# A streaming encoder's FFN loop: weight-block sums moved from GpSimd to Vector, Scalar's order changed, once-a-layer pieces moved to the ends of turns

## Chip, cores and metric

One core of one Trainium2 chip runs the whole program. The metric is the device time of one execution in microseconds (us), lower is better.

## What is computed

One inference step of a 2-layer hybrid encoder over 1088 tokens (1024 of a new stream, 64 of a running one), model width 1024, all in float32. Each layer has three token mixers fed by one input projection, an output projection with a residual, and then the part that this case is about, a SwiGLU FFN of width 2816:

```python
h2 = rmsnorm(x, lp['norm_ffn']) * (1.0 + sc2) + sh2
a, u = jnp.split(h2 @ lp['w_ffn_in'], 2, axis=-1)
x = x + g2 * ((jax.nn.silu(a) * u) @ lp['w_ffn_out'])
```

## The kernel before

**Precision.** TensorE works on float32 data split into two parts: a high part that Scalar makes with a copy, and the rest, a low part that Vector makes by subtracting. Each product then is three passes (`PASSES`: high x high, high x low, low x high). So every weight block costs one Scalar copy (`w_high`, L1706; `out_high`, L1712, for the output weights) and one Vector subtraction (`w_low`, L3198; `out_low`, L3202).

**The FFN in turns.** A layer's FFN is 22 turns: two passes over the tokens (`p` = 0 and 1, 544 tokens each, as two halves of 272) times eleven groups of 256 hidden columns. The document counts the turns 0 to 21 in the first layer and 22 to 43 in the second, from the start of product 1a to the next turn's. In a turn the product of the (1024 x 256) block "a" with the tokens, and the same for block "u", are each done as seven products of half blocks instead of eight (Strassen's scheme in Winograd's form). `PRODUCT` tells for each of the seven its weight set, its set of token sums and its PSUM bank, `PE_ORDER` (L78) the order of the fourteen on TensorE, `BANK_FREE` (L79) what frees each one's bank. A product is 12 matmuls of 272 columns. Then the output part (`part`) adds the (256 x 1024) block of the output weights in 16 pieces x0 to x15 of 6 matmuls; a turn has 264 matmuls in all.

**The seven weight sets.** Sets 0, 3 and 5 are quarters of the raw block in SBUF. Sets 1, 2, 4 and 6 are sums: S1 = q10 + q11, S2 = S1 - q00, S3 = q00 - q10, S4 = q01 - S2. GpSimd makes them (`w_step`, L1039): for u at a turn's begin, for the next turn's a in its middle. Each set's place is shared by a and u (but for set 6) and is free once the product that read it is done (`set_free`). Scalar then copies the high part, Vector subtracts.

**Vector, Scalar and GpSimd in a turn** each run a fixed list, written out in their `group` functions (L1044, L1724, L3277). Besides the weights: Scalar copies product banks to SBUF (`kept`: p1a, u2a, p1u, u3a, u2u, u3u), applies Silu (`gated`, s21a) and copies the hidden activations' high parts (g11 ...). Vector adds two products (`summed`: c11a ...), makes the hidden low parts (h11 ...) and the 16 additions to x (`added`, L3300). GpSimd multiplies Silu(a) by u (`times`, L1050: m11u, m22u, m12u). Every wait is a semaphore; an engine stands at a wait with all that is behind it.

**SyncE** (L699 to L704) loads the raw blocks with one buffer for each of a, output weights and u: block a of the next turn once `l5` of the present one (the low part of set 5, last on Vector's list for that block) is made, then the output block after `f3`, then u.

**Once-a-layer pieces.** They are hooked into single turns by name (`hook`): in turn 0 the rest of the first token sums (T3, T4, B22 and their parts); in turn 1 the squares of the last token chunk with GpSimd's additions; in turn 2 the root; in turns 3 and 4 the normalised second half (`scaled` on Vector, `shifted` on Scalar); in turn 10 the token sums T1, T2, T4 and parts B11, B21 for the second pass; in turn 11 as in turn 0; in turn 12 of the first layer the next layer's squares. `Fori` loops run turns 5 to 9 and 13 to 20. In turn 10 the last sets of block a are left to turn 11.

Of the kernel before, what the change touches and what calls it, by code (L numbers as in the profile page):

```python
# [77 lines left out]
PE_ORDER = ["1a", "5a", "2a", "6a", "1u", "7a", "2u", "5u", "6u", "4a", "7u", "3a", "4u", "3u"]  # L78
BANK_FREE = {"1a": ("ffn_dve", -1, "x12"), "5a": ("ffn_dve", -1, "x14"), "2a": ("ffn_dve", -1, "x13"),  # L79
# [94 lines left out]
def program(nc, io, plan):  # L174
# [340 lines left out]
    with ctx:  # L515
# [211 lines left out]
        def _(pool):  # L727
# [23 lines left out]
            for l in range(DEPTH):  # L751
# [272 lines left out]
                def w_step(b, turn, name, first=False):  # L1024
                    s = st(f"fw{b}_pool")
                    i = int(name[1])
                    to = {1: 1, 2: 2, 3: 4, 4: 6}[i]
                    pool.wait_ge(raw_ld[1 + (b == "u")], w_ready(b, turn))
                    set_free(pool, b, turn, to)
                    if first:  # L1030
                        wait(pool, "wo_pe", l, "o19" if to < 4 else "o21")
                    if i == 2:
                        wait(pool, f"fw{b}_pool", turn, "S1")
                    elif i == 4:
                        wait(pool, f"fw{b}_pool", turn, "S2")
                    x, y, op = {1: (w_quarter(b, 1, 0), w_quarter(b, 1, 1), ALU.add), 2: (w_sum(1, b), w_quarter(b, 0, 0), ALU.subtract),
                                3: (w_quarter(b, 0, 0), w_quarter(b, 1, 0), ALU.subtract),
                                4: (w_quarter(b, 0, 1), w_sum(2, b), ALU.subtract)}[i]
                    s.done(V.tensor_tensor(w_sum(to, b), x, y, op), name)  # L1039

                def w_ready(b, turn):
                    return raw_ready(l, 16 + (b == "u")) + 16 * (turn - 2 * l * NGROUP)

                def group(g, hook=lambda name: None, last=False):  # L1044
# [2410 lines left out]
```

How the kernel before makes its waits and increments, by code:

```python
    def wait(eng, name, turn, step):  # L449
        s = st(name)
        eng.wait_ge(s.sem, s.value(turn, step))
# [73 lines left out]
        @block.sync  # L525
# [7 lines left out]
                    wait(sp, "in_pe", 0, "x0b")  # L533
                sp.dma_start(x_rows(t)[0:TILES[t][1]], rows(xp, xs, t)).then_inc(x_ld[t], 16)
            def load_raw(l, n, src, k):
                r = n % 3
                dst = WR[:, r, 0:k * src.shape[-1]].rearrange("p (k c) -> p k c", k=k)
                sp.dma_start(dst, src).then_inc(raw_ld[r], 16)
            for l in range(DEPTH):
                sp.wait_ge(w_lo, l * SPLIT_N + 1)
                if l:
                    for b in "au":
                        wait(sp, f"fw{b}_dve", last_group(l - 1), "l5")
# [16 lines left out]
                    elif l == 0 and n == 2:  # L563
                        wait(sp, "in_pe", 0, "x5b")
                    load_raw(l, n, wl[:, :, FM_COLS[n]:FM_COLS[n] + 256], 8)
                order = [("t", 0), ("t", 1), ("m", 0), ("t", 2), ("t", 3), ("w", 9), ("w", 10), ("w", 11)]
                for kind, n in order:
                    if kind == "m":
                        wait(sp, "n1_dve", l, "lo27")
                        load_mod(sp, l, n)
                    elif kind == "t":
                        sp.wait_ge(w_lo, lo_val(l, n + 1))
                        at = 0
                        for c, wd in TM_SLOTS[n]:
                            sp.dma_start(WTR[:, n % 2].rearrange("p (k c) -> p k c", k=8)[:, :, at:at + wd],
```

## Time and profile before

| | |
|---|---|
| median of 3 runs | 3280.22 us (3276.21 to 3283.54) |
| the profiled execution's own time | 3277.33 us |
| its span, first to last instruction | 3274.9 us |
| TensorE (PE) busy | 3088.1 us, 94% |
| Vector (DVE) busy | 2203.0 us, 67% |
| Scalar (ACT) busy | 1426.2 us, 44% |
| GpSimd (POOL) busy | 1326.2 us, 40% |
| mean granted TensorE clock | 0.986 |

PE is TensorE's matmul, PEld its weight load, SPq SyncE's queue. Matmuls are pipelined, so PE busy isn't PE at its peak: how long TensorE needs is read from the distance between turns. L1912 is the helper through which all matmuls go. The first layer's FFN begins at 885 us of the span, the second's at 2491 us.

### The profile page before, as it was taken

The numbers are of one execution on the slowest core, as the hardware profiler recorded it, in microseconds if no ns is written. First come the engines' busy times: TensorE is split into PE (matmuls) and PEld (weight loads), VectorE is DVE, ScalarE is ACT, GpSimd is POOL, SyncE is SP. The second block draws the span as 40 slices with busy tenths as digits, with TensorE's granted clock in tenths as the row PEclk, the third lists the DMA queues.
The fourth block names the chain that finished last, engine by engine and source line by source line (L and its number), as shares of the span: only waits on it lengthen the run. The fifth ranks groups of instructions, "written<-read, shape, count | busy, mean of one in ns | idle before, by whom it ended". The sixth has DMA issues, their size and how long they took to land. (4 is left out here: it accounts for less than half of the span.)

```text
span 3274.9 us, 61123 instructions
## 1 busy us (share of the span) xinstructions
PE 3088.1 (94%) x21870; PEld 2768.8 (85%) x21870; DVE 2203.0 (67%) x3741; ACT 1426.2 (44%) x3199; POOL 1326.2 (40%) x1439
## 2 busy tenths in 40 slices
PE   6999998999999998999989999898999999999999
PEld 5997666767999998999989976666699999989999
DVE  5312656656588888888873036665557888888986
ACT  5222345444345444444452234554434544444444
POOL 2213556521354354444421145664213543443442
PEclk8999989999999999999999999999999999999999
DMA  6415811104023222223232263111211232222222
GB/s 220 141 68 178 256 42 56 43 17 133 13 91 104 90 90 87 82 90 102 77 110 99 86 218 101 55 53 29 99 52 52 78 100 93 78 89 96 85 102 93
DMA packets 241018, 307.08 MB, mean 94 GB/s; under 512 B 19705, under 2 KB 206414, under 8 KB 240814
## 3 DMA queue, kind: packets, MB, share of 16 engines
q1 hardware_dynamic: 185900, 227.65, 21.2%
q10 hardware_dynamic: 44354, 45.25, 4.3%
q0 software_dynamic: 10560, 31.44, 2.7%
q8 instruction: 130, 2.13, 0.3%
q14 instruction: 74, 0.61, 0.1%
HBM read 264.74 MB, written 39.56 MB: 93 GB/s over the span
## 5 line engine op out<-in xcount | busy, mean ns | idle before, releaser
L1912 PE MATMUL banks<-act_split,w_sets_first 128*128 128x272 f32 x4224 | 554.8, 290 | 15.3 <-DVE w_sets_first L3198 10.4
L1912 PEld LDWEIGHTS banks<-act_split,w_sets_first 128*128 128x128 f32 x4224 | 542.2, 189 | 19.4 <-DVE w_sets_first L3198 13.7
L1912 PE MATMUL banks<-hidden_split,w_out_split 128*128 128x272 f32 x4224 | 541.5, 288 | 5.0 <-DVE x L3300 3.6
L1912 PEld LDWEIGHTS banks<-hidden_split,w_out_split 128*128 128x128 f32 x4224 | 533.5, 188 | 7.3 <-DVE x L3300 6.0
L1912 PE MATMUL banks<-act_split,w_sets_last 128*128 128x272 f32 x3168 | 429.6, 292 | 35.1 <-ACT product_sums L1731 26.8
L1912 PEld LDWEIGHTS banks<-act_split,w_sets_last 128*128 128x128 f32 x3168 | 409.7, 190 | 46.8 <-issue 35.8
L3300 DVE SCALAR_TENSOR_TENSOR x<-banks,mod,x 128x272 f32<-128x272 f32 (+1 forms) x880 | 346.4, 435 | 76.1 <-PE banks L1912 75.5
L1039 POOL TENSOR_TENSOR w_sums_first<-w_raw 128x512 f32<-128x512 f32 x88 | 143.8, 1634 | 566.6 <-PE banks L1912 565.7
L1912 PE MATMUL banks<-act_split,w_split 128*128 128x384 f32 (+1 forms) x2016 | 344.9, 331 | 11.0 <-DVE act_split L2708 10.7
L1912 PEld LDWEIGHTS banks<-act_split,w_split 128*128 128x128 f32 x2016 | 337.6, 191 | 15.5 <-issue 10.6
L1912 PE MATMUL banks<-w_split_tm,act_split 128*128 128x396 f32 (+1 forms) x1728 | 317.2, 344 | 0.0
L1912 PEld LDWEIGHTS banks<-w_split_tm,act_split 128*128 128x128 f32 (+1 forms) x1728 | 300.9, 182 | 13.2 <-issue 4.0
L1712 ACT ACTIVATE w_out_split<-w_raw 128x512 fp32r<-128x512 f32 x176 | 105.4, 622 | 325.4 <-PE banks L1912 325.4
L3202 DVE TENSOR_TENSOR w_out_split<-w_raw,w_out_split 128x512 fp32r<-128x512 f32 x176 | 228.1, 1296 | 0.0
L1050 POOL TENSOR_TENSOR silu_a<-silu_a,product_sums 128x272 f32<-128x272 f32 x132 | 129.1, 978 | 177.2 <-DVE product_sums L3284 168.5
L3198 DVE TENSOR_TENSOR w_sets_first<-w_sums_first,w_sets_first 128x512 fp32r<-128x512 f32 x176 | 192.7, 1095 | 12.0 <-POOL w_sums_first L1039 8.7
L1912 PE MATMUL banks<-k_t,q_t 98*128 98x512 f32 (+4 forms) x448 | 167.3, 487 | 14.2 <-ACT probs L1405 6.3
L3198 DVE TENSOR_TENSOR w_sets_first<-w_raw,w_sets_first 128x512 fp32r<-128x512 f32 x176 | 130.8, 744 | 72.1 <-ACT w_sets_first L1706 72.1
L2937 DVE COPY_PREDICATED r_p<-r_cst,banks 128x512 f32<-128x512 int32 x126 | 112.8, 895 | 90.6 <-PE banks L1912 76.1
L1912 PE MATMUL banks<-r_qb,r_kb 128*128 128x128 f32 x756 | 137.8, 319 | 29.6 <-issue 9.8
L811 POOL TENSOR_TENSOR r_kb<-r_qkg,r_e 128x192 f32<-128x192 f32 x126 | 81.6, 648 | 203.1 <-ACT r_e L1278 159.6
L1912 PEld LDWEIGHTS banks<-r_qb,r_kb 128*128 128x128 f32 x756 | 98.7, 192 | 75.0 <-issue 40.0
(286 smaller groups left out, 5250.5 us busy)
## 6 DMA issues: line engine op xcount, KB each, us to landing
w_raw<-in_w_ffn_in SPq DMA_DIRECT2D x88, 1024.0 KB, 5.1
w_raw<-in_w_ffn_out SPq DMA_DIRECT2D x44, 1024.0 KB, 5.0
w_mod_front<-in_w_mod ACTq DMA_DIRECT2D x50, 512.0 KB, 6.2
w_mod_third<-in_w_mod ACTq DMA_DIRECT2D x26, 512.0 KB, 5.7
z_token_major<-z_stage POOLq DMA_DIRECT2D x64, 198.0 KB, 2.2
r_qkg<-z_feature_major SPq DMA_DIRECT2D x16, 576.0 KB, 4.2
r_v<-z_token_major SPq DMA_DIRECT2D x16, 512.0 KB, 3.7
w_raw<-in_w_o SPq DMA_DIRECT2D x8, 1024.0 KB, 6.3
```

The costliest lines, as they stand in the source:

```text
L811: rstep(V.tensor_tensor(blk(rKB[:, r])[:, :, :, 0:b], blk(rZ[:, g % 2, 3:6])[:, :, :, 0:b], blk(ee)[:, :, :, 0:b], ALU.mult), f"k{g}_{lv}")
L1039: s.done(V.tensor_tensor(w_sum(to, b), x, y, op), name)
L1050: s.done(V.tensor_tensor(SIL[:, i], SIL[:, i], PU[:, j], ALU.mult), f"m{name}u")
L1712: st("fwo_act").done(S.activation(WO2[:, 0, 512 * j:512 * j + 512], WR[:, 0, 512 * j:512 * j + 512], ACT.Copy), f"f{j}")
L1912: return T.matmul(out, lhsT, rhs, start=start, stop=stop, skip_group_check=True)
L2937: rstep(V.copy_predicated(out, mask.unsqueeze(1).broadcast_to([P, 8, 64 // b, b]), src), f"m{g}_{lv}")
L3198: st(f"fw{b}_dve").done(V.tensor_tensor(lo, src, hi.bitcast(F32), ALU.subtract), f"l{i}")
L3202: st("fwo_dve").done(V.tensor_tensor(WO2[:, 1, 512 * j:512 * j + 512], WR[:, 0, 512 * j:512 * j + 512], WO2[:, 0, 512 * j:512 * j + 512].b ...
L3300: ins = V.scalar_tensor_tensor(out=x, in0=ps[OUT_ROT[q % 6]][:, a0:a1], scalar=MOD[:, 40 + d, m:m + 1], in1=x, op0=ALU.mult, op1=ALU.add)
```

## The change

- GpSimd's `group` keeps only the three `times`; the eight sums a turn go to Vector as `w_add`, with the same waits.
- Scalar: `w_high` u1 and u3 and the bank copy u2a stand ahead of s11a, u2 and u6 ahead of p1u, and the next turn's a0 right behind p1u, ahead of out_high 3 and u3a (before: after g11). The other a copies move forward too; s22a goes behind u2u.
- Vector: a new order, with the a sums and most a splits ahead of the output part.
- On TensorE product 2u goes ahead of 7a.
- Once-a-layer pieces: squares, GpSimd's adds and Scalar's `shifted` at the end of their turn, Vector's `scaled` after x3, x6, x9, x12; in turns 0 and 11 the splits a6 and a5 after c11u (before: after u3), T4's low part after c22a, B22's after a1; in turn 10 the passes spread over the turn.

The diff, cut to what matters:

```diff
-PE_ORDER = ["1a", "5a", "2a", "6a", "1u", "7a", "2u", "5u", "6u", "4a", "7u", "3a", "4u", "3u"]
+PE_ORDER = ["1a", "5a", "2a", "6a", "1u", "2u", "7a", "5u", "6u", "4a", "7u", "3a", "4u", "3u"]
...
-                    for name in ("S1", "S2"):
-                        w_step("u", g, name)
-                    hook("S2")
-                    for name in ("S4", "S3"):
-                        w_step("u", g, name)
                     times("11", 0, 0)
...
                     times("22", 3, 2)
...
                     times("12", 1, 0)
...
+                for i in range(2):
+                    group(g0 + i)
+                last_adds()
...
+                for i in range(NGROUP - 1, NGROUP + 2):
                     group(g0 + i)
-                group(g0 + NGROUP + 1, next_adds)
+                if l + 1 < DEPTH:
+                    norm_adds(l + 1, 0)
...
                     w_high("u", g, 0)
                     hook("u0")
                     out_high(g, 2)
+                    w_high("u", g, 1)
                     w_high("u", g, 3)
+                    kept("u2a", "6a", 1, ("ffn_dve", g - 1, "c12a"))
                     gated("11", 0)
-                    w_high("u", g, 1)
-                    kept("u2a", "6a", 1, ("ffn_dve", g - 1, "c12a"))
+                    w_high("u", g, 2)
+                    w_high("u", g, 6)
+                    kept("p1u", "1u", 0, ("ffn_dve", g, "c11a"))
+                    if not last:
+                        w_high("a", g + 1, 0)
                     out_high(g, 3)
-                    kept("p1u", "1u", 0, ("ffn_dve", g, "c11a"))
-                    w_high("u", g, 2)
                     kept("u3a", "7a", 2, ("ffn_pool", g - 1, "m22u"))
-                    w_high("u", g, 6)
-                    gated("22", 3)
                     w_high("u", g, 4)
                     hidden("11", 0, ("ffn_pool", g, "m11u"))
                     if not last:
-                        w_high("a", g + 1, 0)
+                        w_high("a", g + 1, 3)
+                        w_high("a", g + 1, 1)
                     kept("u2u", "6u", 0, ("ffn_pool", g, "m11u"))
+                    gated("22", 3)
...
+                def w_add(b, turn, name, first=False):
+                    to = {"S1": 1, "S2": 2, "S3": 4, "S4": 6}[name]
+                    dve.wait_ge(raw_ld[1 + (b == "u")], w_ready(b, turn))
+                    set_free(dve, b, turn, to)
...
+                    if name in ("S2", "S4"):
+                        own(f"fw{b}_dve", turn, "S1" if name == "S2" else "S2")
...
+                    st(f"fw{b}_dve").done(V.tensor_tensor(w_sum(to, b), x, y, op), name)
...
                     hook("start")
+                    out_low(g, 0)
                     w_low("u", g, 0)
-                    hook("u0")
-                    out_low(g, 0)
+                    w_add("u", g, "S1")
+                    out_low(g, 1)
                     summed("c11a", 0, 0, 1, ("ffn_act", g, "p1a"), ("ffn_pe", g, "2a"))
-                    out_low(g, 1)
                     w_low("u", g, 3)
                     hook("u3")
+                    w_add("u", g, "S2")
+                    w_add("u", g, "S4")
+                    w_low("u", g, 1)
+                    w_low("u", g, 2)
+                    w_low("u", g, 6)
+                    summed("c11u", 0, 0, 4, ("ffn_act", g, "p1u"), ("ffn_pe", g, "2u"))
+                    if not last:
+                        w_low("a", g + 1, 0)
                     out_low(g, 2)
-                    w_low("u", g, 1)
+                    w_add("u", g, "S3")
                     summed("c22a", 3, 2, 2, ("ffn_act", g, "u3a"))
...
                     out_low(g, 3)
                     if not last:
-                        w_low("a", g + 1, 0)
-                    hook("a0")
+                        w_add("a", g + 1, "S1")
+                    w_low("u", g, 4)
+                    hidden("11", 0)
+                    if not last:
+                        w_add("a", g + 1, "S2")
+                        w_low("a", g + 1, 3)
+                        w_low("a", g + 1, 1)
+                    hook("a1")
                     w_low("u", g, 5)
+                    if not last:
+                        w_add("a", g + 1, "S3")
                     summed("c22u", 2, 2, 5, ("ffn_act", g, "u3u"))
...
+                    for q in range(1, 16):
                         added(q)
-                        if not last and q in (5, 8) or q in lows:
-                            w_low("a", g + 1, {5: 2, 8: 4, 10: 6, 13: 5}[q])
+                        if q == 5 and late:
+                            w_low("a", g + 1, 5)
...
                 def set_end(p, name):
                     if name == "start":
                         h_add(p, "T3")
-                    elif name == "u0":
+                    elif name == "u3":
                         h_low(p, "T3")
-                    elif name == "u3":
-                        h_low(p, "T4")
+                    elif name == "c11u":
                         for i in (6, 5):
                             w_low("a", (2 * l + p) * NGROUP, i)
                     elif name == "c22a":
+                        h_low(p, "T4")
+                    elif name == "a1":
                         h_low(p, "B22")
...
                 def pieces_of(k0):
                     def at(name):
-                        if name in ("u0", "u3", "c22a", "c11u"):
+                        if name in ("x3", "x6", "x9", "x12"):
...
                 def turn_over(name):
                     if name == "h11":
                         h_add(1, "T1")
-                    elif name == "a0":
+                    elif name == "a1":
                         h_add(1, "T2")
-                    elif name == "c12a":
+                    elif name == "h22":
                         h_low(1, "B11")
-                    elif name == "h12":
+                    elif name == "x3":
                         h_low(1, "T1")
-                    elif name == "x4":
+                    elif name == "x6":
                         h_add(1, "T4")
-                    elif name == "x7":
+                    elif name == "x9":
                         h_low(1, "B21")
-                    elif name == "x11":
+                    elif name == "x12":
                         h_low(1, "T2")
```

## Rows read from the trace of the kernel before

**Rows 1.** The page, part 1: busy time (share of the span) and instructions per engine

```profile
PE 3088.1 (94%) x21870; PEld 2768.8 (85%) x21870; DVE 2203.0 (67%) x3741; ACT 1426.2 (44%) x3199; POOL 1326.2 (40%) x1439
```

**Rows 2.** Windows: stretch, length; busy PE, PEld, DVE, ACT, POOL; granted clock; DMA share, GB/s

```profile
885.31:927.94 42.63, 36.61 (x266) 36.00 (x265) 40.45 (x59) 19.45 (x36) 19.26 (x11) 0.92 0.23 75
927.94:964.44 36.50, 34.23 (x266) 33.41 (x265) 29.65 (x45) 17.83 (x40) 22.54 (x18) 1.00 0.25 87
...
998.15:1035.02 36.87, 34.17 (x266) 33.35 (x265) 32.23 (x58) 20.16 (x45) 15.69 (x11) 1.00 0.26 87
1035.02:1072.31 37.29, 34.44 (x267) 33.40 (x265) 33.03 (x58) 18.85 (x44) 15.55 (x11) 1.00 0.25 86
1206.48:1240.03 33.55, 33.46 (x267) 33.25 (x265) 29.12 (x46) 15.18 (x32) 15.15 (x11) 1.00 0.28 94
1240.03:1281.19 41.16, 34.62 (x267) 33.41 (x265) 34.00 (x50) 20.21 (x38) 16.68 (x11) 1.00 0.23 77
1281.19:1319.67 38.48, 34.28 (x264) 33.43 (x265) 35.67 (x59) 16.70 (x33) 14.65 (x11) 1.00 0.25 83
1319.67:1357.44 37.77, 34.68 (x269) 33.61 (x267) 31.43 (x52) 18.32 (x41) 23.57 (x18) 1.00 0.25 84
...
899.50:902.40 2.90, 2.86 (x13) 2.89 (x14) 2.90 (x5) 2.22 (x4) 0.00 (x0) 0.50 0.02 6
```

**Rows 3.** Timeline of turn 9: start, length, engine, line, operation, [idle before <-releaser]

```profile
1208.28 0.40 ACT L1731 ACTIVATE product_sums<-banks 128x272 f32<-128x272 f32 x1 [0.44 <-PE banks L1912]
...
1218.54 1.86 DVE L3198 TENSOR_TENSOR w_sets_last<-w_sums_last,w_sets_last 128x512 fp32r<-128x512 f32 x2
1218.79 1.06 POOL L1050 TENSOR_TENSOR silu_a<-silu_a,product_sums 128x272 f32<-128x272 f32 x1 [1.07 <-DVE product_sums L3284]
...
1224.07 0.68 DVE L3198 TENSOR_TENSOR w_sets_last<-w_raw,w_sets_last 128x512 fp32r<-128x512 f32 x1
...
1224.87 3.06 PEld L1912 LDWEIGHTS banks<-act_split,w_sets_last 128*128 128x128 f32 x24 [0.30 <-issue]
...
1231.60 1.72 DVE L3300 SCALAR_TENSOR_TENSOR x<-banks,mod,x 128x272 f32<-128x272 f32 x4
```

**Rows 4.** Groups by line over the whole span: count | busy, mean ns | idle before

```profile
L3202 DVE TENSOR_TENSOR w_out_split<-w_raw,w_out_split 128x512 fp32r<-128x512 f32 x176 | 228.1, 1296 | 0.0
L3198 DVE TENSOR_TENSOR w_sets_first<-w_sums_first,w_sets_first 128x512 fp32r<-128x512 f32 x176 | 192.7, 1095 | 12.0 <-POOL w_sums_first L1039 8.7 <-POOL w_sums_last L1039 2.7
...
L1039 POOL TENSOR_TENSOR w_sums_first<-w_raw 128x512 f32<-128x512 f32 x88 | 143.8, 1634 | 566.6 <-PE banks L1912 565.7 <-DMA w_raw<-in_w_ffn_in 0.9
...
L1712 ACT ACTIVATE w_out_split<-w_raw 128x512 fp32r<-128x512 f32 x176 | 105.4, 622 | 325.4 <-PE banks L1912 325.4
```

**Rows 5.** Timeline before and in turn 0

```profile
877.95 1.28 DVE L3198 TENSOR_TENSOR w_sets_first<-w_raw,w_sets_first 128x512 fp32r<-128x512 f32 x2
...
899.54 3.06 PE L1912 MATMUL banks<-act_split,w_sets_last 128*128 128x272 f32 x12 [4.90 <-ACT product_sums L1731]
...
901.64 0.39 SPq L539 DMA_DIRECT2D w_raw<-in_w_ffn_in  x1
```

**Rows 6.** Timeline: turn 1, then turn 3, then turn 4

```profile
956.63 1.91 POOL L1086 TENSOR_TENSOR norm_sum_n<-norm_sum_n,norm_sq 128x320 f32<-128x320 f32 x2
...
1003.60 1.28 ACT L1736 ACT_TABLE_LOAD   x1
...
1048.56 0.62 DVE L3188 SCALAR_TENSOR_TENSOR h_second<-x,gain_scale,norm_rs_last 128x208 f32<-128x208 f32 x2
```

**Rows 7.** Timeline of turns 10 and 11

```profile
1258.97 1.28 DVE L3222 TENSOR_TENSOR act_f<-h_second,act_f 128x1088 f32<-128x1088 f32 x1
...
1261.03 34.16 SPq L539 DMA_DIRECT2D w_raw<-in_w_ffn_in  x2
...
1262.34 3.24 PE L1912 MATMUL banks<-act_split,w_sets_last 128*128 128x272 f32 x24 [3.13 <-ACT product_sums L1731]
...
1299.97 1.29 POOL L1039 TENSOR_TENSOR w_sums_first<-w_raw 128x512 f32<-128x512 f32 x1 [0.41 <-DMA w_raw<-in_w_ffn_in]
```

More of the change, by code:

```diff
@@ L1022, in add, with group @@
                                f"ad{c}_{d}")
[L1024 to L1044, printed above, removed]
+                def group(g):
                     s = st("ffn_pool")
@@ L1703, in w_high @@
                     else:
[L1704 removed]
+                        wait(act, f"fw{b}_dve", turn, {1: "S1", 2: "S2", 4: "S3", 6: "S4"}[i])
                         src = w_sum(i, b)
@@ L1779, in group @@
                     if not last:
-                        w_high("a", g + 1, 2)
+                        w_high("a", g + 1, 5)
                     hidden("12", 1, ("ffn_pool", g, "m12u"))
-                    if not last:
-                        for i in (6, 4, 5):
-                            w_high("a", g + 1, i)
                     hook("end")
@@ L1836, in squares @@
                 def squares(name):
-                    at = ("p1a", "s11a", "s22a", "g11", "u2u", "g21", "g22", "g12")
-                    if name in at:
-                        last_square(at.index(name))
+                    if name == "end":
+                        for d in range(KT8):
+                            last_square(d)
                 def rooted(name):
@@ L1846, in at @@
                     def at(name):
-                        if name in ("s11a", "p1u", "g11", "u2u"):
-                            k = k0 + ("s11a", "p1u", "g11", "u2u").index(name)
-                            for u in range(2):
-                                shifted(k, 1, u)
+                        if name == "end":
+                            for k in range(k0, k0 + 4):
+                                for u in range(2):
+                                    shifted(k, 1, u)
                     return at
                 def turn_over(name):
-                    if name in ("u3a", "g11", "u2u", "s21a"):
-                        h_high(1, {"u3a": "B11", "g11": "B21", "u2u": "T1", "s21a": "T2"}[name])
+                    if name in ("p1u", "u3a", "u3u", "end"):
+                        h_high(1, {"p1u": "B11", "u3a": "B21", "u3u": "T1", "end": "T2"}[name])
                 def again(name):
@@ L1860, in next_squares @@
                 def next_squares(name):
-                    at = ("p1a", "s11a", "s22a", "g11", "u2u", "g21", "g22", "g12")
-                    if l + 1 < DEPTH and name in at:
-                        normed_square(l + 1, 0, at.index(name))
+                    if l + 1 < DEPTH and name == "end":
+                        for d in range(KT8):
+                            normed_square(l + 1, 0, d)
                 def ending(name):
@@ L3262, in _ @@
                 project(19)
-                for i in (0, 3):
-                    w_low("a", g0, i)
+                w_low("a", g0, 0)
+                w_add("a", g0, "S1", True)
+                w_add("a", g0, "S2", True)
                 h_low(0, "B11")
@@ L3275, in _, with group @@
                 h_low(0, "T2")
-                def group(g, p, hook=lambda name: None, last=False, lows=(10, 13)):
+                def group(g, p, hook=lambda name: None, last=False, late=True):
                     s = st("ffn_dve")
```

97 lines of the change are left out of this document (40 added, 57 removed), and 4 rows, old and new, of the table BANK_FREE.

## Prediction, made before the changed kernel was run

> Times inside a turn count from its first product's start. Products are named as in `PE_ORDER`, sets as in `w_set`.
>
> **What bounds the kernel now.** First the page: TensorE is busy 94% of the span [rows 1], so Vector or Scalar work that is removed only counts where TensorE waits. So I cut the FFN into its 44 turns and read the length of each [rows 2]. Every turn has 264 matmuls of the same size. A turn of the loops (turn 9) takes 33.55 us. Its only wait is the 0.30 us before 4u [rows 3]; of that about 0.25 is excess in the pace of the matmuls, so a turn without waits would take 33.3. The other rows show what the once-a-layer work costs: turn 0 is 9.3 longer than that, turn 1 3.2, turn 3 3.6, turn 4 4.0, turn 10 7.9, turn 11 5.2, turn 12 4.5. The second layer has the same pattern within 0.5 us, except that its turn 12 has nothing extra. So about 75 us stand at the edges and 7 us (29 turns of 0.25) in the steady turns. More than these 80 us the change can't give.
>
> **The price of a sum.** A GpSimd sum takes 1634 ns [rows 4], and while it runs a Vector operation with both inputs in SBUF stands still: the split of a sum takes 1095 ns in the mean [rows 4], two take 1.86 us beside a GpSimd operation [rows 3], and 1.28 without one [rows 5]. Alone it is 0.68 [rows 3], and 0.60 from start to start in a row. No row shows a sum on Vector. It has the shape and operands of the split, so I take 0.60; the bounds are 0.60 and the contended 1.095. Eight per turn are 4.8 us, of which the lost contention pays most: (1296-680)x4 for the output weights [rows 4] and (1095-680)x4 for the split of sums are 4.1 us. Vector is busy 29.1 of 33.55 us in turn 9 [rows 2], so it ends about where it was. The Trainium skill, page VectorE: DVE Perf Modes, section "The DRAIN you can't avoid", says that the next operation doesn't start until the pipe is empty. By it a sum costs 0.68; six operations stand between product 2u and the last sum that matters, and 7u would come some 0.15 us late. The 1.28 us for two [rows 5] speak against it.
>
> **A steady turn after the change.** I walk Vector's new order with 0.60 for each 128x512, 0.35 to 0.4 for the 272-wide ones, and 0.28 from a product's end to who waits for it (1a ends at 1.52, its copy starts at 1.80 [rows 3]). With one product each 1.52 us: `w_low` u0 ends 3.4, c11a 5.5, u3 6.1 (2u starts at 7.6), S2 and S4 at 7.7, u1 8.3, u2 8.9, u6 9.5, c11u 9.9. GpSimd's product takes 1.06 [rows 3] and holds a0 up to 11.0; then out_low 11.6, S3 12.2, c22a 12.6, out_low 13.2, S1 of the next set 13.8. Scalar's `w_high` a1 waits for that S1: 14.4, then its copy u2u ends at 14.8, and 7u, which needs the bank, starts at 15.2: slack 0.35. Vector goes on: u4 14.4, h11, S2, a3, a1, u5 at 17.2, and 4u starts at 18.3: slack 1.0 where it waits now. h21 is there at 22.1, needed at 22.9. In the output part the 16 additions take 0.41 each (four in 1.72 [rows 3]) against TensorE's 0.76: no wait. So 29 turns give 0.25 each: **7.2 us**. The swap of 7a and 2u gives 7a's copy and sum 1.5 us more and costs nothing here, since u3 is early.
>
> **Scalar's copies ahead of its waits, pieces at the ends.** Scalar stands idle before a turn's first copy for 325.4 us in 44 turns [rows 4], 7.4 us each. Turn 1: squares and GpSimd's adds (two in 1.91 [rows 6]) go there, eight of about 1.1 end before the next turn: 3.2 saved. Turn 3: the table load of 1.28 [rows 6] no longer stands ahead of u2a, which 7a waits for; it makes u2u late by 0.7. The pieces of the norm on Vector (0.41 like the additions of that width, and 0.55 for the second half in two parts, 0.62 to its end [rows 6]) come between additions: four pairs are 3.9 us, so x14 comes 0.4 late for the next turn's 5a. Turn 3 becomes 34.4, 2.5 saved. Turn 4 has the 0.4 alone: 3.6 saved. Turn 10: the 1088-wide passes cost 1.28 alone [rows 7] and, like all others, some 0.08 less in a row, 1.2. Two stand before u5, which ends at 20.0: 4u waits 1.8 instead of 3.13 [rows 7], 7u no more; four among the additions put x12 at 35.7, and turn 11 starts at 35.8 instead of 41.2: 5.4 saved. Turn 12, first layer: the adds end about when the norm's matmul wants them, a wait of 0.5: 3.9 saved. The sum over both layers is 6.4+5.0+7.2+10.8+3.9 = **33.3 us**.
>
> **What the same move costs.** At turn 0 and turn 11, `w_low` of a5 and a6 is late by design, and SyncE loads the next "a" block only after a5's. Now that load is issued 13.6 us into turn 11 (the first of the pair at 1261.03 is the "u" block, the second ends its issue at 1295.19) and lands some 5 us later: GpSimd's sum waits for it until 1299.97 [rows 7]. Nobody on Scalar waits, because `w_high` of the next a0 stands behind u3a and g11. After the change it stands right behind p1u, ahead of out_high 3, u3a and u4. Turn 11: Vector starts at 2.4 (x15), T3, a4, out_low, u0, S1, out_low, c11a, u3, T3's low part 9.2, S2, S4, u1, u2, u6, c11u 12.6, a6 and a5 13.8. The load lands at 19.1; Scalar and Vector both stand until then. a0 20.4, out_low, S3, c22a 22.0, T4's low part 23.2: 4a starts at 23.35 instead of the 14.3 when TensorE is free, **a wait of 9 us**. Behind it B22's low part ends at 28.4, which 3a waits for, and the output part begins at 33.1, 11.8 later than in a clean turn. So 45.1 instead of 38.5: 6.6 lost. Turn 0: the pieces before it no longer run beside GpSimd's sums, which pays for the four sums on Vector; 7a no longer waits 4.90 [rows 5]; l5 comes at 901.1, the load lands at 906.5 (issue now 901.64 [rows 5]), and the same chain begins the output part at 920.5 instead of 915.9: 4.6 lost. Twice both: **22.4 us**. A wait of 9 us will also lower TensorE's clock: after the 4.90 us one the granted clock is 0.50 [rows 2], the 1.2 GHz level. Two slow products of 2.7 instead of 1.5 fit almost into the next wait (for 3a, 1.45 us); 0.25 each, 1 us in all. The Trainium skill, TensorE: Matmul & The Clock Gate, "HAM oscillation", has it that idle gaps bring the clock down each time; by it all four waits do, which is what I count.
>
> **Sum.** 7.2+33.3-22.4-1.0 = 17 us off the profiled execution's 3277.3: 3260. The median of the three runs is 2.9 above that, so 3263.
>
> **The rivals.**
> *The late load isn't in the way* (0.11). If the a block is there when Scalar comes to it, turns 0 and 11 lose their 5.5 us of standing each: 22 off, 3241. Against it: a5's release and the 5 us are in the rows, and nothing shortens them.
> *The edges give nothing* (0.15). In turns 3, 4 and 10 Vector has more work than room, and pieces put among additions make those late, as x already is in turn 10 of before. If half of the 33 us stays away, 3280: within 0.2%, about what a measurement of this kernel can tell from no change.
> *The steady turn gets a new wait* (0.09). Place: 7u, through S1 of the next set, `w_high` a1 and u2u on Scalar. Five sums stand before it, the slack is 0.35. At 0.60 each there is no wait; with d more per sum 7u is 5d-0.35 late, in 29 turns. From d = 0.2 on the gain is gone (19 us); at 0.3, well below the contended price (1.095), it is 33 us: 3296, slower. For it: two-input operations are what GpSimd's remaining products hold up. Against it: with the sums gone GpSimd runs 3 operations of 1 us a turn instead of 11.
> *The clock* alone moves nothing: were the slow products never hidden, four times 2.6 make 10 us, 3273, within my own case.
> That the change doesn't do what it says I give nothing: GpSimd's sums are gone from the code.
>
> **How the numbers follow.** My case has 0.65, its own range 3248 to 3276. It lies on the faster side but for its last edge, 0.03, which goes to "same". Faster by over 0.2% (6.6 us): 0.62+0.11 and a little of the second rival, 0.75; same 0.15; slower 0.10. The range reaches to the first rival and to the half gain: 3240 to 3283.
>
> **What the changed profile would show.** Right: loop turns of 33.3 without a wait before 4u; Vector's sums at 0.68 each, splits of sums and output weights near 0.68; GpSimd down to 3 operations a turn; turn 10 near 36; in turns 0 and 11 a TensorE wait of about 9 us before 4a, with Scalar's a0 copy waiting for the DMA of w_raw, and a low clock after it. Wrong: a wait before 7u in every loop turn, sums of 0.9 or more, turns 3 and 4 not under 36, or turn 11 under 40.

## The result, and the profile after

The changed kernel takes **3255.92 us** (median of 4 runs, 3253.46 to 3256.22), the kernel before 3279.19 us (4 runs, 3276.21 to 3283.54): a ratio of **0.9935**, with a 95% interval of 0.9923 to 0.9947. The forecast was 3263, with a range of 3240 to 3283 and 0.75 for "faster": right in sign, inside its range, and 7 us short of the gain. The profiled execution took 3256.1 us, its span is 3253.6 against 3274.9.

Part 1 of the page of the kernel after, as in [rows 1]:

```profile
PE 3073.5 (94%) x21870; PEld 2768.3 (85%) x21870; DVE 2205.9 (68%) x4093; ACT 1448.5 (45%) x3199; POOL 759.6 (23%) x1087
```

GpSimd lost 352 instructions and 567 us of busy time. Vector took the 352 over, and its busy time rose by 3 us only: the sums cost it 253 us, and what it already did became 250 us shorter. That is the exchange that the prediction worked out. Groups of the kernel after by line (lines have moved: L3172 is the split of a set, before L3198; L3176 that of the output weights, before L3202; L3166 a sum on Vector; L1030 GpSimd's product, L1664 Scalar's `w_high`):

```profile
L3172 DVE TENSOR_TENSOR w_sets_last<-w_sums_last,w_sets_last 128x512 fp32r<-128x512 f32 x176 | 143.3, 814 | 0.0
L3176 DVE TENSOR_TENSOR w_out_split<-w_raw,w_out_split 128x512 fp32r<-128x512 f32 x176 | 141.5, 804 | 4.4 <-ACT w_out_split L1670 3.1
L1030 POOL TENSOR_TENSOR silu_a<-silu_a,product_sums 128x272 f32<-128x272 f32 x132 | 118.9, 900 | 1395.7 <-DVE product_sums L3262 1395.7
L3172 DVE TENSOR_TENSOR w_sets_first<-w_sums_first,w_sets_first 128x512 fp32r<-128x512 f32 x176 | 116.8, 683 | 1.0 <-ACT w_sets_first L1664 1.0
L1664 ACT ACTIVATE w_sets_first<-w_raw 128x512 fp32r<-128x512 f32 x176 | 109.9, 625 | 35.5 <-DMA w_raw<-in_w_ffn_in 32.9 <-PE banks L1871 1.7
L3166 DVE TENSOR_TENSOR w_sums_last<-w_raw,w_sums_first 128x512 f32<-128x512 f32 x88 | 71.4, 812 | 3.3
L3166 DVE TENSOR_TENSOR w_sums_first<-w_raw 128x512 f32<-128x512 f32 x88 | 60.2, 684 | 0.0
```

Three of the four sums cost 684 to 688 ns. S4 (`w_sums_last<-w_raw,w_sums_first`) costs 812 in the mean: 42 of its 88 run beside a GpSimd product, at 942 each, the other 46 take 692. The split of a first-half sum fell from 1095 to 683 ns and that of the output weights from 1296 to 804 [rows 4]; what is above 683 in the first and second row is those groups' share beside GpSimd's remaining products (about 1.21 us for 44 and 1.23 for 38 of the 176; 0.68 to 0.69 for the others). Windows of the kernel after, turns 0, 1, 3, 4, 8, 10, 11 and 12 of the first layer, columns as in [rows 2]:

```profile
881.32:929.30 47.98, 36.53 (x266) 35.35 (x265) 38.99 (x64) 19.60 (x36) 2.82 (x3) 0.89 0.26 88
929.30:962.48 33.18, 33.18 (x266) 33.18 (x265) 29.48 (x53) 19.01 (x40) 9.25 (x10) 1.00 0.29 96
996.20:1029.95 33.75, 33.41 (x266) 33.22 (x265) 30.99 (x62) 20.48 (x43) 2.83 (x3) 1.00 0.28 95
1029.95:1063.13 33.18, 33.18 (x266) 33.18 (x265) 31.88 (x66) 20.22 (x45) 2.83 (x3) 1.00 0.29 97
1162.67:1195.85 33.18, 33.18 (x266) 33.18 (x265) 29.03 (x53) 15.55 (x32) 2.66 (x3) 1.00 0.29 95
1229.03:1265.06 36.03, 33.79 (x266) 33.23 (x265) 32.99 (x55) 20.09 (x38) 2.44 (x3) 1.00 0.18 59
1265.06:1310.78 45.72, 36.09 (x265) 35.70 (x265) 37.88 (x70) 17.77 (x34) 2.83 (x3) 0.89 0.28 93
1310.78:1344.31 33.53, 33.53 (x269) 33.40 (x267) 30.27 (x63) 19.60 (x41) 10.22 (x10) 1.00 0.29 95
```

Timeline of the loop turn 8 (from 1162.67): c11u, S1 of the next set, and Scalar's copy u2u.

```profile
1172.16 0.43 DVE L3262 TENSOR_TENSOR product_sums<-product_sums,banks 128x272 f32<-128x272 f32 x1
...
1175.85 0.68 DVE L3166 TENSOR_TENSOR w_sums_first<-w_raw 128x512 f32<-128x512 f32 x1
...
1177.10 0.38 ACT L1689 ACTIVATE product_sums<-banks 128x272 f32<-128x272 f32 x1
```

In a loop turn TensorE is busy for all of its 33.18 us. Turns 1 and 4 are as short as that, turns 3 and 12 nearly so, and turn 10 became 5.1 us shorter. Turns 0 and 11 alone became longer, by 5.3 and 7.2 us, at a granted clock of 0.89. The two layers together, all 44 turns: 25.4 us lost in turns 0, 11, 22 and 33, 45.6 us won in the others, **20.2 us** net.

The timeline of turn 11 (it starts at 1265.06) shows where its time went:

```profile
1277.22 0.43 DVE L3262 TENSOR_TENSOR product_sums<-product_sums,banks 128x272 f32<-128x272 f32 x1
...
1279.60 0.38 SPq L539 DMA_DIRECT2D w_raw<-in_w_ffn_in  x1
...
1284.59 0.63 ACT L1664 ACTIVATE w_sets_first<-w_raw 128x512 fp32r<-128x512 f32 x1 [8.15 <-DMA w_raw<-in_w_ffn_in]
1285.13 0.61 ACT L1670 ACTIVATE w_out_split<-w_raw 128x512 fp32r<-128x512 f32 x1
1285.26 0.69 DVE L3172 TENSOR_TENSOR w_sets_first<-w_raw,w_sets_first 128x512 fp32r<-128x512 f32 x1 [5.83 <-ACT w_sets_first L1664]
...
1287.41 1.29 DVE L3204 TENSOR_TENSOR act_split<-act_f,act_split 128x1088 fp32r<-128x1088 f32 x1
...
1288.80 10.09 PE L1871 MATMUL banks<-act_split,w_sets_last 128*128 128x272 f32 x60 [9.35 <-DVE act_split L3204]
```

The next "a" block's load is issued 14.5 us into the turn and Scalar's a0 gets it 5.0 us later. Scalar stood 8.15 us for it, then Vector 5.83; the split of T4, which product 4a reads, comes last, and TensorE stands 9.35 us.

### The profile page after: what moved, and what is told of

Its sections match the earlier page's. It is cut to its first block and busy times, and to the rows that moved or that the text cites. A ratio compares the mean times of both kernels' runs of the same rounds, so it can differ in the third digit from the quotient of the medians.

```text
span 3253.6 us, 60947 instructions
## 1 busy us (share of the span) xinstructions
PE 3073.5 (94%) x21870; PEld 2768.3 (85%) x21870; DVE 2205.9 (68%) x4093; ACT 1448.5 (45%) x3199; POOL 759.6 (23%) x1087
## 5 line engine op out<-in xcount | busy, mean ns | idle before, releaser
L1871 PE MATMUL banks<-act_split,w_sets_last 128*128 128x272 f32 x3168 | 422.9, 293 | 41.5 <-DVE act_split L3204 37.8
L1030 POOL TENSOR_TENSOR silu_a<-silu_a,product_sums 128x272 f32<-128x272 f32 x132 | 118.9, 900 | 1395.7 <-DVE product_sums L3262 1395.7
L3278 DVE SCALAR_TENSOR_TENSOR x<-banks,mod,x 128x272 f32<-128x272 f32 (+1 forms) x880 | 356.5, 438 | 63.8 <-PE banks L1871 44.3
L1871 PEld LDWEIGHTS banks<-w_split_tm,act_split 128*128 128x128 f32 (+1 forms) x1728 | 300.8, 182 | 13.2 <-issue 4.0
L3172 DVE TENSOR_TENSOR w_sets_first<-w_raw,w_sets_first 128x512 fp32r<-128x512 f32 x176 | 122.0, 693 | 78.8 <-ACT w_sets_first L1664 78.8
L1871 PE MATMUL banks<-w_raw,c_t 128*128 128x512 f32 (+3 forms) x352 | 156.3, 567 | 4.0 <-ACT c_t L1300 4.0
L1664 ACT ACTIVATE w_sets_last<-w_sums_last 128x512 fp32r<-128x512 f32 x176 | 111.6, 634 | 100.5 <-DVE w_sums_last L3166 98.1
L1689 ACT ACTIVATE product_sums<-banks 128x272 f32<-128x272 f32 x264 | 103.5, 392 | 104.7 <-PE banks L1871 102.0
L2648 DVE TENSOR_TENSOR w_split_tm<-w_raw_tm,w_split_tm 128x3168 fp32r<-128x3168 f32 x8 | 27.7, 3457 | 179.7 <-ACT w_split_tm L1078 179.7
```

Of the source, the lines that this page charges most:

```text
L1030: s.done(V.tensor_tensor(SIL[:, i], SIL[:, i], PU[:, j], ALU.mult), f"m{name}u")
L1664: s.done(S.activation(hi, src, ACT.Copy), f"h{i}")
L1689: s.done(S.activation(PU[:, i], ps[bank][:, 0:HALF], ACT.Copy), name)
L1871: return T.matmul(out, lhsT, rhs, start=start, stop=stop, skip_group_check=True)
L2648: V.tensor_tensor(WT[:, 1 - j % 2, 1], WTR[:, j % 2], WT[:, 1 - j % 2, 0].bitcast(F32), ALU.subtract).then_inc(w_lo, 1)
L3172: st(f"fw{b}_dve").done(V.tensor_tensor(lo, src, hi.bitcast(F32), ALU.subtract), f"l{i}")
```

## The experiments

Unless said otherwise, each starts from the kernel after. "In the turns" is the summed difference of the lengths of the 44 FFN turns in the two profiles. It tells more than the whole time does: turn 0 starts at 881.32 after the change and at 887.57 in e12's kernel, though the two have the same instructions ahead of it. Each ratio is to runs of the kernel before that were made beside that experiment (their medians are 3275.0 to 3279.1), so it can differ a little from the quotient of the times given here.

**e1: late load, one step, a0 behind g11.** In turns 0, 11, 22 and 33 (Vector's split a0 and its sum S1 go behind h11 there, not shown):

```diff
+                    if fresh:            # behind hidden("11", ...)
+                        w_high("a", g + 1, 0)
```

> After the change with one step moved, in turns 0 and 11 of both layers alone: Scalar's copy a0 of the next turn's block comes behind its fourth square root-like product g11 instead of ahead of the output part 3, and Vector's split a0 and the sum S1 come behind h11. My theory (the late load of raw-a holds Scalar, and with it the out part 3, u3a and u4, so that product 4a waits 9.6 us): the out part 3 no longer waits for the load, u4 comes some 4 us earlier, 4a waits about 5 us instead of 9.6, and each of the four turns is 4 us or so shorter, 16 to 18 us in all: about 3238 us. Rival (4a waits for something else, the throttle or the load of raw-u): these turns stay at 46 to 48 us and the time at 3256.

Measured: 3250.88 us, ratio to the kernel before 0.9921 [0.9904, 0.9937]; 12.1 us less in the turns, not 16 to 18. The timeline of its turn 11 (from 1268.06):

```profile
1285.27 2.51 PE L1873 MATMUL banks<-act_split,w_sets_last 128*128 128x272 f32 x12 [2.83 <-issue]
...
1287.64 1.15 ACT L1664 ACTIVATE w_sets_first<-w_raw 128x512 fp32r<-128x512 f32 x2 [3.04 <-DMA w_raw<-in_w_ffn_in]
...
1290.17 0.38 ACT L1689 ACTIVATE product_sums<-banks 128x272 f32<-128x272 f32 x1
...
1290.69 7.48 PE L1873 MATMUL banks<-act_split,w_sets_last 128*128 128x272 f32 x38 [2.92 <-ACT product_sums L1689]
```

4a's wait fell to 2.83 us, so the load was what it waited for. But Scalar now stands for the same load ahead of its copy u2u, and 7u waits 2.92 us. The wait was handed on to the next product.

**e2: late load, whole chain.** Both engines' work on the next "a" block, in the same four turns, behind all that 4a, 7u and 3a wait for:

The code is shortened: `u3a` stands for its `kept(...)` call, and so on; Vector's list is changed in the same manner.

```diff
+                    if fresh:
+                        out_high(g, 3); u3a; w_high("u", g, 4); g11; u2u; s22; s21a; w_high("u", g, 5)
+                        w_high("a", g + 1, 0); u3u; w_high("a", g + 1, 3); ...
```

> After the change, with all work on the next turn's a-block in turns 0 and 11 put behind the work that product 4a and 4u wait for (Scalar: out part 3, u3a, u4, g11, u2u, s22, s21a, u5, then a0 and the rest; Vector in the same manner). My theory: Scalar and Vector meet no wait for the late load before u4, so 4a waits 2 to 3 us instead of 9.6; each of the four turns is 7 to 9 us shorter, 28 to 35 us in all: 3221 to 3228 us. If the late load is needed by the next turn's first products before it can be turned into its pieces, the loss moves to the start of turns 1 and 12, up to 3 us each: 3233. Rival (the load is not what 4a waits for): 3256.

Measured: **3224.42 us**, 0.9844 [0.9827, 0.9860]; 31.7 us less in the turns (7.3, 8.3, 8.8 and 7.4 in the four). Almost nothing came back behind them: turns 12 and 34 are 0.1 us longer, turns 1 and 23 are not. The timeline of its turn 11 (from 1262.43) at 4a:

```profile
1278.28 1.28 DVE L3229 TENSOR_TENSOR act_split<-act_f,act_split 128x1088 fp32r<-128x1088 f32 x1
...
1279.65 7.77 PE L1896 MATMUL banks<-act_split,w_sets_last 128*128 128x272 f32 x60 [2.83 <-issue]
```

What is left there is Vector's queue: 4a starts when the split of T4 ends.

**e3: late load, issued earlier.**

```diff
                     elif name == "u3":
                         h_low(p, "T3")
-                    elif name == "c11u":
                         for i in (6, 5):
```

> After the change, with Vector's splits a6 and a5 in turns 0 and 11 put back from c11u to u3, where the kernel before has them; the load of raw-a is issued behind a5, so it starts some 3.4 us earlier. My theory: the load lands 3.4 us earlier, u4 and 4a follow, each of the four turns is 3 to 3.5 us shorter, less up to 1 us for product 5u, whose u5 path the two splits (0.6 us each) now delay: 8 to 14 us in all, 3242 to 3248 us. Rival (the load is not what 4a waits for): 3256 or up to 4 us more.

Measured: 3243.50 us, 0.9901 [0.9885, 0.9918]; 16.2 us less in the turns, more than the 8 to 14 expected (3.3 in turn 0, 4.2 to 4.3 in each of the others). SyncE's queue in its turn 11 (from 1263.72):

```profile
1274.11 0.38 SPq L539 DMA_DIRECT2D w_raw<-in_w_ffn_in  x1
```

The load is issued 10.4 us into the turn instead of 14.5, and turn 11 is 4.3 us shorter: nearly microsecond for microsecond. The expectation took off up to 1 us for 5u; 5u did wait 1.1 us, but that was hidden in what 4a waited anyway.

**e4: the swap of products, undone.**

```diff
-PE_ORDER = [..., "1u", "2u", "7a", "5u", ...]
+PE_ORDER = [..., "1u", "7a", "2u", "5u", ...]
```

> After the change, with the one swap of products undone: 7a ahead of 2u again. The sums stay on Vector. In the prediction the swap was costed at nothing in a steady turn. Two theories. First: nothing, 3256. Second: 2u ends one product later, so the accumulator that it fills is read later by Vector (c11u and the combining of it), and Vector, now filled with the sums, hands over the piece for 7u late: up to 0.8 us in each of 38 turns or so, 23 to 30 us in all, 3279 to 3286.

Measured: 3303.89 us, 1.0086 [1.0069, 1.0103], **slower than the kernel before**; 44.9 us more in the turns, not 23 to 30, and 34.31 us for a loop turn. The second theory has the direction right and half the size. One such turn (from 1175.02):

```profile
1185.80 0.44 DVE L3262 TENSOR_TENSOR product_sums<-product_sums,banks 128x272 f32<-128x272 f32 x1 [1.21 <-PE banks L1871]
...
1189.50 0.68 DVE L3166 TENSOR_TENSOR w_sums_first<-w_raw 128x512 f32<-128x512 f32 x1
...
1191.18 1.03 PE L1871 MATMUL banks<-act_split,w_sets_last 128*128 128x272 f32 x6 [0.86 <-ACT product_sums L1689]
```

c11u starts 10.8 us into the turn, after the change 9.5. Everything behind it on Vector moves along, S1 of the next set from 13.2 to 14.5, and with it `w_high` a1, u2u and 7u.

**e5: the sums back on GpSimd, all else as changed** (`w_step` of the kernel before in GpSimd's turn, Vector's `w_add` out; GpSimd's order is not quite the old one, since u's S3 comes behind m11u instead of ahead of it).

> After the change, with the sums of the weight blocks back on GpSimd and all else as changed: the swap of 7a and 2u, Scalar's copies ahead of its waits, the pieces at the ends of turns. One theory: the gains at the edges of passes (25 of the 33 us forecast) come from the order alone and stay; a steady turn loses its 0.36 us again, 29 times 10 us, and may lose more since a sum takes 1.1 us there and two-input operations of both engines hold each other up: 3262 to 3275 us. Other theory: the new order of Scalar wants the sums earlier than GpSimd has them (three 1.1 us sums stand ahead of m11u, and S1 of the next set behind it), so Scalar waits in the middle of the turn ahead of u2u and 7u is late by 1 us or more in each of 38 turns: 3290 us or above.

Measured: **3398.64 us**, 1.0367 [1.0337, 1.0397]; 144.2 us more in the turns, 36.23 us for a loop turn. Groups by line of GpSimd's sums and of the matmuls that read the last sets:

```profile
L1039 POOL TENSOR_TENSOR w_sums_first<-w_raw 128x512 f32<-128x512 f32 x88 | 152.4, 1732 | 551.2 <-PE banks L1902 534.5 <-DMA w_raw<-in_w_ffn_in 16.7
...
L3191 DVE TENSOR_TENSOR w_sets_first<-w_sums_first,w_sets_first 128x512 fp32r<-128x512 f32 x176 | 120.7, 688 | 210.4 <-POOL w_sums_last L1039 161.2 <-POOL w_sums_first L1039 49.2
...
L1902 PE MATMUL banks<-act_split,w_sets_last 128*128 128x272 f32 x3168 | 444.7, 299 | 110.7 <-ACT product_sums L1720 63.8 <-DVE act_split L3223 37.0 <-DVE w_sets_last L3191 8.1
```

A sum takes 1.5 to 1.7 us there, not the 1.1 that the expectation took, and the new order wants it at once. 7u waits 1.8 us and the output part another 1.1 in each loop turn. That is the second theory. The steady turn gains nothing from the order without the faster sums. The edges do: turns 1, 3, 4, 10, their like in the second layer and turn 12 stand 39.5 us above a loop turn of their own kernel before the change, 18.3 us here and 7.2 after the change. So about 21 of the 32 us that these turns came nearer to a loop turn came with the order, even with the sums on GpSimd.

**e6: the sum S1 of "a" three times.**

```diff
+                    if b == "a" and name == "S1":
+                        for r in ("S1r", "S1s"):
+                            st("fwa_dve").done(V.tensor_tensor(w_sum(to, b), x, y, op), r)
+                            own("fwa_dve", turn, r)
```

> After the change, with the sum S1 of each a-block computed three times, one after the other, in every turn (the same sum in the same place; nothing is left out). It puts 1.2 to 1.4 us more on Vector ahead of the sum that Scalar's a1 waits for, behind which u2u stands, which 7u waits for. My walk gave this path 0.35 us of slack in a steady turn: 7u then waits 0.85 to 1.05 us more in each of some 38 turns, 32 to 40 us in all: 3287 to 3296 us, and 4u no more than that. Rival (Vector has more slack than that, since 1.2 us a turn is less than a fifth of its idle time): below 3262 us.

Measured (one run): 3320.55 us; 58.9 us more in the turns, not 32 to 40; a loop turn takes 34.46 us, 1.28 more. One of them, from 1178.70:

```profile
1191.88 1.41 DVE L3168 TENSOR_TENSOR w_sums_first<-w_raw 128x512 f32<-128x512 f32 x2
1193.32 0.69 DVE L3170 TENSOR_TENSOR w_sums_first<-w_raw 128x512 f32<-128x512 f32 x1
```

The two extra sums hold S1 up by 1.44 us, and 7u waits 1.18 of it: the slack is 0.26 us, not 0.35. e4 says nearly the same (1.3 late, 1.02 waited). The misses of the expectation: each extra sum cost 0.72 us and not 0.60 to 0.70, since each of the three waits for the one ahead; the matmul behind a wait starts 0.1 us late as well; the extra sums counted in 41 turns and not in 38; and turns 0 and 22 lost 2.7 us each.

**e7: the norm's pieces back in the middle of turns 3, 4, 25 and 26** (Vector's at c11a, u3, c22a, c11u; Scalar's at s11a, p1u, g11, u2u).

> After the change, with the once-a-layer pieces of the second pass's norm back where the kernel before has them: Vector's scaled pieces at c11a, u3, c22a and c11u, Scalar's shifted pieces at s11a, p1u, g11 and u2u, in turns 3, 4, 25 and 26. In the prediction their move, with the sums' move, saves 2.5 us of turn 3 and 3.6 us of turn 4, twice. Measured after the change these turns take 33.75 and 33.18 us, before 36.9 and 37.3. If the pieces' place is the cause: each of the four turns is 3 to 4.1 us longer, 12 to 16 us in all: 3267 to 3270 us. If it is the sums on Vector that relieved these turns: 3256 to 3260 us. Since a pair of pieces on Vector is about 1 us and the slack there 0.35, more than 16 us would say that Vector, now with the sums, is worse off than before.

Measured: 3273.60 us (10 runs), 0.9993 [0.9982, 1.0004], no faster than the kernel before; 17.5 us more in the turns, a little above the 12 to 16 expected, turn 3 at 38.0 and turn 4 at 37.7 us. Its turn 3:

```profile
1011.54 0.49 DVE L3147 SCALAR_TENSOR_TENSOR act_high_f<-x,gain_scale,norm_rs_last 128x272 f32<-128x272 f32 x1
...
1012.16 0.51 ACT L1649 ACTIVATE act_high_f<-act_high_f,mod 128x272 f32<-128x272 f32 x1
1012.57 0.69 ACT L1649 ACTIVATE h_second<-h_second,mod 128x208 f32<-128x208 f32 x2
...
1014.87 1.47 PE L1871 MATMUL banks<-act_split,w_sets_last 128*128 128x272 f32 x5 [3.19 <-ACT product_sums L1689]
```

The pieces stand ahead of S1 on Vector and ahead of u2u on Scalar, and 7u waits 3.2 us. Pieces at hooks in the middle of the turn cost turn 3 less in the kernel before, 3.3 us over a loop turn (36.87 us [rows 2]) against 4.8 here. Vector had no sums there, but its order was another too, and no run separates the two.

**e12: Scalar's waits ahead of its copies again** (s11a ahead of the copies of set 1 and u2a, s22 ahead of u4).

> After the change, with Scalar's waits put ahead of its copies again where the kernel before has them so, and nothing else undone: the copy of set 1 and u2a behind the Silu s11a, and the Silu s22 ahead of u4 instead of behind u2u. Two theories. First: these places give nothing in a steady turn (Scalar is busy 45%), 3252 to 3258 us. Second: s22 waits for Vector's c22a, which in the new order comes 12.6 us into the turn, so Scalar has u4, g11, a3, a1 and u2u some 0.8 to 1.0 us later than now; with the slack of 0.24 us that e6 showed ahead of 7u, 7u waits 0.6 to 1.2 us in each of 38 turns: 22 to 45 us in all, 3277 to 3300 us.

Measured: 3270.31 us (10 runs), 0.9973 [0.9959, 0.9987]; 9.3 us more in the turns, a loop turn at 33.48 us with 0.2 us of wait ahead of 7u. That is a cost, by the path that the second theory names, but well under half of its smallest size: it falls between the two ranges. Scalar in such a turn (from 1170.42), s22 and then u2u:

```profile
1183.10 0.43 ACT L1694 ACTIVATE silu_a<-silu_a 128x272 f32<-128x272 f32 x1 [1.43 <-DVE silu_a L3262]
...
1185.32 0.38 ACT L1689 ACTIVATE product_sums<-banks 128x272 f32<-128x272 f32 x1
```

Behind s22 the copy u4 starts 0.68 us later than after the change. Some 0.2 us of that is made up at a1, which had waited for S1 of the next set, so u2u is 0.47 us late, and the slack takes 0.26 of it.

**e11: the swap alone, in the kernel before.**

> The kernel before, with the swap of products 7a and 2u alone. e4_product_order showed that the swap is worth 46 to 50 us once the sums are on Vector. Theory one: it is worth nothing without them, since the kernel before waits at 4u and not at 7u: 3275 us, as before, within 5. Theory two: 7a one product later makes its copy u3a on Scalar and the sum c22a later, on which GpSimd's order and u2u hang, as in e5_sums_gpsimd, where steady turns took 36.2 us: a wait of 0.5 us or more ahead of 7u in 40 turns, 20 us or more in all: above 3295 us.

Measured: 3306.81 us, 1.0088 [1.0066, 1.0110]; 27.7 us above the kernel before beside it. In the profile the turns take 35.2 us more, but the profiled execution was 11 us slower than the median of its runs (3317.77 us), so that is the upper end. It is slower, as the second theory says, but at another place. A turn from 1178.05:

```profile
1186.35 1.77 DVE L3198 TENSOR_TENSOR w_sets_first<-w_sums_first,w_sets_first 128x512 fp32r<-128x512 f32 x1
...
1188.91 0.40 ACT L1731 ACTIVATE product_sums<-banks 128x272 f32<-128x272 f32 x1 [2.02 <-PE banks L1912]
...
1189.34 0.44 DVE L3284 TENSOR_TENSOR silu_a<-product_sums,banks 128x272 f32<-128x272 f32 x1 [1.21 <-ACT product_sums L1731]
1189.69 1.02 DVE L3198 TENSOR_TENSOR w_sets_first<-w_sums_first,w_sets_first 128x512 fp32r<-128x512 f32 x1
...
1190.84 1.77 PE L1912 MATMUL banks<-act_split,w_sets_first 128*128 128x272 f32 x12 [0.54 <-DVE w_sets_first L3198]
```

The wait is ahead of 6u, for the split of set 2, not ahead of 7u, and 4u's wait is longer than before too. The rows show why set 2 comes later. Its split stands right behind c22a on Vector, c22a waits for Scalar's copy u3a, and u3a for product 7a: u3a starts 10.9 us into the turn instead of 9.4, and the split at 11.6 instead of 10.35.

**e9: Vector in the order of use.** e2's kernel, and in its four turns:

```diff
                     summed("c11u", ...)
-                        a6, a5; out_low(g, 2); u S3; c22a; T4; out_low(g, 3); u4; h11; B22; u5
+                        a6, a5; T4; u S3; c22a; u4; B22; h11; u5; out_low(g, 2); out_low(g, 3)
```

> The kernel of e2_fresh_order, and in its four first turns of a pass Vector's work between c11u and c22u put in the order in which TensorE wants it: the splits a6 and a5, the split of T4, the sum S3, c22a, u4, the split of B22, h11, u5, and the two output parts last. In e2's turn 11 the split of T4 began at 1278.28 us, with an output part, the sum S3 and c22a (0.6, 0.6 and 0.35 us) between it and the two splits of a; product 4a waited 3.1 us for it. My theory: 4a comes 1.5 us earlier in each of the four turns, of which 7u takes back up to 0.4: 4 to 6 us in all, and up to 4 us more where the shorter wait leaves TensorE's clock alone (in turns 0 and 22 to 33 of e2 some 16 matmuls ran at 227 ns behind it): 3216 to 3220 us. Rival (the wait is set by Scalar's u3a or its copy of B22): e2's 3224 again.

Measured: 3222.16 us, 0.9839 [0.9818, 0.9860]; 36.5 us less in the turns than after the change. That is 4.7 less than in e2's kernel, inside the 4 to 6 expected; the whole time came down by 2.3 us only and missed the 3216 to 3220. Its turn 11:

```profile
1271.82 1.28 DVE L3229 TENSOR_TENSOR act_split<-act_f,act_split 128x1088 fp32r<-128x1088 f32 x1
...
1273.20 1.76 PE L1896 MATMUL banks<-act_split,w_sets_last 128*128 128x272 f32 x12 [1.28 <-issue]
```

**e10: and turn 10.** e9's kernel, with T2's addition later and its split after the last x.

> The kernel of e9_splits_in_order_of_use, and in turns 10 and 32 Vector's addition T2 (1.2 us) put behind h22 instead of ahead of the split u5 that product 4u waits for, and the split of T2 behind the last addition of the turn instead of ahead of the last three. e9's turns 10 take 36.04 us (4u waits 1.77 us, the next turn's first product 1.05 us) and 5a in turn 11 waits 0.56 us. Theory: 4u waits 0.6 instead of 1.77 us, 5a no more; the split moved away gives Vector 1.2 us ahead of the addition x12, which pays for T2's coming 1.2 us later, so the wait of 1.05 stays: 1.7 us less per pass end, 3 to 4 us in all: 3218 to 3220 us. Rival (Vector is full from 4u to the end of the turn, so what 4u gains the next turn's first product waits for): 3221 to 3223 us.

Measured: 3219.53 us, 0.9824 [0.9805, 0.9844], 36.5 us less in the turns, the same as e9's. The whole time would fit the theory (3218 to 3220), but the turns fit the rival: 4u waits 0.4 instead of 1.6 us, and the output part waits for Vector instead; turn 10 is 36.03 us here and 36.04 in e9's kernel, and turn 11 is as long in both. The 2.6 us between the two medians lie within the scatter of these five runs (3215.6 to 3224.1), so against e9's kernel this is no difference. Both are 1.6% to 1.8% faster than the kernel before, and about 1% faster than the change.

## Why the prediction was right

**The steady turn: right place, size off.** The forecast walk holds closely: c11u ends 9.9 us into turn 8 and u2u at 14.8, both as forecast, 7u starts at 15.13 (forecast 15.2) and no wait is left. The term "29 turns give 0.25 each: 7.2 us" measured 0.365 in 27 turns, 9.9 us (turns 2 and 24, which it counted too, did not change). The missing part is not in the wait: before, the matmuls around 4u's start lie 0.38 and 0.23 us apart, against 0.125 in the kernel after. The second one I had left out.

**A sum on Vector, 0.60 start to start: right, with one exception.** The sums and splits that stand in a row without a wait start 0.60 to 0.61 us apart at 0.68 each. An operation that waits for the one ahead starts later: S4, which needs S2, starts 0.73 us behind it in the loop turn. The rule of the Trainium skill that the prediction set beside it (VectorE: DVE Perf Modes, "The DRAIN you can't avoid") would have them 0.68 apart; the trace disagrees, except where there is such a wait. The same page's section "Two Vector instructions with no wait between them", which I had passed over, lets an operation start before the one ahead has finished where both begin in the same quarter of the partitions, as all of these do: by that one the trace agrees. The slack ahead of 7u was 0.26 us (e6) and not 0.35.

**"The swap costs nothing": true, and the wrong question.** I gave the swap a price of nothing and no value. After the change it is worth 45 us in the turns (e4); alone, in the kernel before, it costs 28 us by the medians and 35 by the turns of the profiled executions (e11). The walk had the answer: c11u can't run before 2u ends, 1.5 us later without the swap, and the slack behind it was 0.35. I never walked the turn with the old order.

**The edges: right, 33.3 us forecast, 35.7 measured.** Turns 1 and 23 gave 6.6 us (6.4 forecast), 3 and 25 6.3 (5.0), 4 and 26 8.2 (7.2), 10 and 32 10.4 (10.8), turn 12 4.2 (3.9). Turn 3 came better since the pieces among the additions didn't make x14 late. e7 shows that the places of the pieces are the cause in turns 3, 4, 25 and 26. Turns 1, 10 and 12 and their like have no run of their own: e5 says that most of their gain comes with the order and the places, but not which step of it.

**The late load: right.** Turn 11 was forecast at 45.1 us with a wait of 9 us at 4a; it took 45.7 with 9.35. The four turns lost 25.4 us against 22.4 and 1.0 for the clock. The slow products cost about what was forecast: 3a starts 0.1 to 0.5 us behind the split of B22 that it waits for. e1, e2 and e3 took the cause apart: the stand is Scalar's and Vector's, for the load; it follows the issue of the load one to one, and ordering past it gives back more than it cost. The rival "the late load isn't in the way" is excluded.

**The sum.** 45.6 less 25.4 is 20.2 us in the turns, where the prediction had 40.5 less 23.4, 17.1. So the terms missed by 2.7 and 2.4 us on the one side and by 2.0 on the other, and part of that cancelled. The span fell by 21.3. Of the 7 us between 3263 and 3255.9 about 4 are the sum's (3 in the turns, 1 outside them), and 3 come from the step from the profiled execution to the median: it was taken as 2.9 us up, as before, and was 0.2 down.

Three figures of the prediction don't come out of its own rows, and none moves the forecast. The edges add up to 71 us and not 75 (twice 37.7, less 4.5). The last turn of each layer, 2.8 and 5.1 us above a loop turn, is left out of that sum and didn't change. And a wait with two slow products costs 2.4 us by its own 2.7 instead of 1.5, where the last rival says 2.6.

**The rivals.** "The steady turn gets a new wait" at 7u didn't occur, but its price was real: e4, e6 and e12 each made it, with no more than 1.4 us of delay, and 0.26 us was all the slack there was. It deserved more than its 0.09. "The edges give nothing" didn't occur either: e7 shows that it would have in turns 3 and 4, had the pieces stayed in the middle.

## What to carry to other kernels

When work moves from one engine to another, the order of the work around it is part of the price. Undoing any one of the four parts that were tried (e4, e5, e7, e12) cost 9 to 144 us of a gain of 20, and the swap alone made the kernel before 28 us slower. So walk the turn with each part left out, and compare the slack with the size of each step.

A step on a block that is still being loaded should stand behind everything that the present turn needs, on every engine that has it in its queue. Moving one step (e1) only hands the wait to the next product; moving all of them (e2, e9) gave more than the whole change.

## What the runs showed of the hardware that was not expected

**TensorE's clock after a wait.** Windows of the turns 0, 11, 22 and 33 in e2's kernel, each with a wait of 3.0 us ahead of 4a (from start to start, less the 0.125 of a matmul; the idle time in a row comes out some 0.15 shorter), and the slow stretch of turn 0:

```profile
886.06:926.69 40.63, 35.96 (x266) 34.94 (x265) 38.13 (x64) 19.32 (x36) 3.46 (x3) 0.96 0.26 85
1262.43:1299.81 37.38, 34.00 (x265) 33.41 (x265) 36.58 (x67) 17.68 (x35) 3.47 (x3) 1.00 0.30 96
2464.65:2503.78 39.13, 34.46 (x267) 33.44 (x265) 38.13 (x64) 19.33 (x36) 3.46 (x3) 1.00 0.26 87
2839.53:2878.21 38.68, 35.44 (x265) 34.87 (x265) 36.56 (x67) 17.53 (x35) 3.46 (x3) 0.96 0.28 93
...
906.50:909.00 2.50, 2.50 (x13) 2.50 (x13) 1.64 (x3) 0.69 (x2) 0.00 (x0) 0.50 0.84 261
```

The same wait brought the clock to the 1.2 GHz level (0.50) for about 15 matmuls twice, 0.227 us apart instead of 0.125, and twice not. In e1's kernel it did so in three of four. After 9.5 us, in the kernel after, it fell each time; after the 1.4 us of e9's kernel never.

**Vector beside GpSimd.** In e11's kernel one 128x512 split took 1.77 us beside a GpSimd sum (the row at 1186.35), another 0.68 without. The Trainium skill, page SBUF — State Buffer, section "Who interferes with whom", has it that the two engines share a port pair under an exclusive lock. The trace agrees with a lock between them: what moved to Vector (352 operations of 0.72 us in the mean, 253 us) raised its busy time by 3 us in all, because the splits that stay there no longer stand beside GpSimd's sums.
